# A hybrid decoder layer: the recurrence's scores, turns and outputs on four quadrants of TensorE, and the first input slab computed bank by bank

## The chip, the cores and the metric

The kernel is one launch on one core of a Trainium2 chip. The metric is the device time of that launch in microseconds (us), taken as the median of several runs. The engines are named as the profile names them: PE is TensorE's matmuls and PEld its weight loads, DVE is VectorE, ACT ScalarE, POOL GpSimd, and SP the queue that issues DMAs.

## What is computed

One layer on 1024 tokens of width 1024, all in float32. The input is projected by `w_in`; its columns feed an RWKV-7 group (8 heads of 64, a recurrence over the tokens) and an attention group (8 heads of 64, causal); both results go through `w_out`, a normalisation, a feed-forward part of width 4096 and a second normalisation. The part at issue is the recurrence, one state of 64 x 64 per head:

```python
def step(S, inp):
    r_t, w_t, k_t, v_t, kk_t, a_t = inp
    sa = jnp.einsum('bhvk,bhk->bhv', S, -kk_t)
    S = (S * w_t[:, :, None, :]
         + sa[..., :, None] * (kk_t * a_t)[:, :, None, :]
         + v_t[..., :, None] * k_t[:, :, None, :])
    y = jnp.einsum('bhvk,bhk->bhv', S, r_t)
    return S, y
```

## The kernel before

**The stages.** `input_projection` transposes x on PE (L375), splits it into a high and a low float32r part (`x_hi` by ACT in L483, `x_lo` by DVE in L753), and makes 20 slabs of 128 columns of `x @ w_in`, two per trip. `mla` is the attention, `rwkv_chunks` the recurrence, `mix_ffn` the rest. Every engine has one stream of instructions in each stage, in an order written out by hand, with semaphores between them; PE runs nearly without idle time in all stages.

**The first slab.** The tokens are transposed in two groups of 512. Group g of tile kt goes into PSUM bank kt, from which ACT and then DVE read it. `slab` (L382 to L392) takes two banks, one for each half of the tokens: for each kt three products (high by high, high by low, low by high) into each bank, 48 matmuls in all. Before the first slab PE waits at L379 and L380 for all 16 pieces of `x_lo` and `x_hi`. The slab's banks are 0 and 1.

**The recurrence.** The 1024 tokens are cut into 16 chunks of 64. The 8 heads lie as 4 tiles (`c`, RT = 4) of two halves (`p`): head 2c on partitions 0 to 63, head 2c+1 on 64 to 127 (`own[p]`). Every matmul is 64 x 64 by 64 columns in float32 and leaves two records for the weight load and two for the matmul. Its operands lie on the partitions of its half, and its result goes to the same partitions of a PSUM bank: so half 0 works on the quadrant of the array with rows and columns 0 to 63, half 1 on the one with rows and columns 64 to 127, and the loops alternate between them.

A stage m works on chunk n = m - 1 (`chain`) and prepares chunk m (`ahead`). PE's order in `stage` (L1725 to L1745) is: `product` into B_T1 (8 matmuls, L1721, tile low_t), `rhs_step` (16, L1633 and L1636), `scores_step` (24, L1684 to L1690), `sa_step` (8, L1645), `product` into B_X (8, L1721, tile product), `transposes` (24, L1703, L1706 and L1714), `state_step` (16, L1655 and L1658), `y_step` (24, L1666 to L1672). That is 128 matmuls, so 256 records a stage.

`rhs_step` waits for the scores masked by DVE (`sc_ready`), for v (`v_ready`), for the new state (`state_ready`), and for `y_out`, since its bank B_RY is also the bank of y: `y_leave` (L1776 to L1778) copies y out of it on ACT in one instruction. `tokens_step` (L1780 to L1786) takes the transposes out of two banks in two ACT instructions (v, then b and k). On DVE `mask_step` (L1836 to L1845) takes the scores out of two banks in two instructions, between `rhs_out` (L1820) and `merged` (L1834), which reads bank B_X and updates the inverse; `state_out` (L1824, L1828) follows.

SP loads three matrices for each chunk (`inv_t`, `inv`, `low_t`, two halves each, six DMAs, L1612) into one of three buffer sets; the loads for chunk m are issued after `sa_step` of stage m - 2, and PE's first product of stage m waits for them. At m = 3 four other transfers are issued ahead of the six.

Of the kernel before, what the change touches and what calls it, by code (L numbers as in the profile page):

```python
# [17 lines left out]
ALU = mybir.AluOpType  # L18
# [6 lines left out]
P = 128  # L25
D = 1024
S = 1024
KT = D // P
TT = S // P
HALF = 512  # L30
# [146 lines left out]
def input_projection(nc, mem, k, t, x, w_in, positions):  # L177
# [68 lines left out]
    with ExitStack() as ctx:  # L246
# [119 lines left out]
        def _(pe):  # L366
            mm = nc.tensor.matmul
            pe.wait_ge(consts_in, 16)
            for g in range(2):
                for tt in range(4):  # L370
                    pe.wait_ge(x_in[4 * g + tt], 16)
                    for kt in range(KT):
# [72 lines left out]
            for n in range(TRIPS):  # L445
# [3 lines left out]
                if n in (5, 6):  # L449
                    pe.wait_ge(keys_rooted, n - 4)  # L450
                if n == 6:
                    slab(n, 0, 5, key_sums((2, 3), 1, 6))
                else:
                    slab(n, 0)
# [1075 lines left out]
def rwkv_chunks(nc, mem, k):  # L1530
# [46 lines left out]
    Y0 = RT  # L1577
    cols = lambda c: slice(c * CH, (c + 1) * CH)
    view = lambda bank, n=RT, at=0: ps[:, bank, at * CH:(at + n) * CH].rearrange("p (c n) -> p c n", n=CH)
    now = lambda m: slice(m * CH, (m + 1) * CH)  # L1580

    with ExitStack() as ctx:
# [38 lines left out]
        def _(pe):  # L1621
# [40 lines left out]
            def y_step(n):  # L1662
                q, a = n % 2, n % 3
                for c in range(RT):
                    for p in range(2):
                        mm(ps[own[p], B_RY, cols(Y0 + c)], state[q][own[p], c, :], rd[a][own[p], c, :],  # L1666
                           start=True, stop=False)
                    for p in range(2):
                        mm(ps[own[p], B_RY, cols(Y0 + c)], v_tok[q][own[p], c, :], ks[q][own[p], c, R, :],
                           start=False, stop=False)  # L1670
                    for p in range(2):
                        last = mm(ps[own[p], B_RY, cols(Y0 + c)], u[own[p], c, :], bs[q][own[p], c, :],  # L1672
                                  start=False, stop=True)
                last.then_inc(y_mm, 1)

            def scores_step(m):
                q, a = m % 2, m % 3
                if m >= 1:
                    pe.wait_ge(kd_ready, m)
                    pe.wait_ge(rd_ready, m)  # L1680
                    pe.wait_ge(sc_ready, m)
                for c in range(RT):
                    for p in range(2):
                        mm(ps[own[p], B_KS, cols(2 * c + A_)], kd[q][own[p], c, :], kk_all[own[p], c, now(m)],  # L1684
                           start=True, stop=True)
                    for p in range(2):
                        mm(ps[own[p], B_KS, cols(2 * c + R)], kd[q][own[p], c, :], rd[a][own[p], c, :],
                           start=True, stop=True)
                    for p in range(2):
                        last = mm(ps[own[p], B_B, cols(c)], beta[own[p], c, now(m)], rd[a][own[p], c, :],  # L1690
                                  start=True, stop=True)
                last.then_inc(scores_mm, 1)

            def transposes(m):
# [6 lines left out]
                for c in range(RT):  # L1701
                    for p in range(2):
                        mm(ps[own[p], B_BKT, cols(B * RT + c)], beta[own[p], c, now(m)], k.eye[own[p], :],  # L1703
                           start=True, stop=True)
                    for p in range(2):
                        mm(ps[own[p], B_BKT, cols(K * RT + c)], kd[q][own[p], c, :], k.eye[own[p], :],  # L1706
                           start=True, stop=True)
                if m == 0:
# [3 lines left out]
                for c in range(RT):  # L1712
                    for p in range(2):
                        last = mm(ps[own[p], B_V, cols(c)], hT[own[p], T_V + c, now(m)], centre[own[p], :],  # L1714
                                  start=True, stop=True)
# [38 lines left out]
        def _(act):  # L1754
# [21 lines left out]
            def y_leave(n):  # L1776
                act.wait_ge(y_mm, n + 1)
                A(y_all[:, :, now(n)], view(B_RY, at=Y0), ACT.Copy).then_inc(y_out, 1)  # L1778

            def tokens_step(m):  # L1780
                act.wait_ge(tr_done, m + 1)
                if m >= 2:
                    act.wait_ge(y_mm, m - 1)
                A(v_tok[m % 2][:], view(B_V), ACT.Copy).then_inc(v_ready, 1)
                A(bk_tok[m % 2][:].rearrange("p a c n -> p (a c) n"), view(B_BKT, 2 * RT), ACT.Copy)\
                    .then_inc(tok_ready, 1)  # L1786

# [17 lines left out]
        def _(dve):  # L1805
# [30 lines left out]
            def mask_step(m):  # L1836
                q = m % 2
                dve.wait_ge(scores_mm, m + 1)
                if m >= 2:
                    dve.wait_ge(y_mm, m - 1)  # L1840
                both = mask[:].rearrange("p (o n) -> p o n", o=1).to_broadcast([P, RT, P])
                until = mask[:, CH:P].rearrange("p (o n) -> p o n", o=1).to_broadcast([P, RT, CH])
                V.tensor_tensor(ks[q][:].rearrange("p c a t -> p c (a t)"),
                                ps[:, B_KS, :].rearrange("p (c n) -> p c n", n=P), both, ALU.mult)
                V.tensor_tensor(bs[q][:], view(B_B), until, ALU.mult).then_inc(sc_ready, 1)  # L1845

# [1328 lines left out]
```

## Time and profile before

| | us |
|---|---|
| median of 3 runs (1405.64 to 1410.1) | 1407.78 |
| the profiled execution | 1404.29 |
| its span, first to last instruction | 1402.5 |
| PE busy in the span | 1351.1 |
| DVE busy | 905.5 |
| ACT busy | 454.5 |

A row of a timeline is: start, time covered, engine, line, operation, out<-in, shapes, count, and in brackets the idle time of the engine before it with what ended it. The mean granted clock of TensorE over the span is 0.988 of its full 2.4 GHz. The profiled execution's time is its span and 1.8 us around it.

### The profile page before, as it was taken

What the parts mean: (1) busy time and instruction counts of PE and PEld (TensorE: products, weight loads), DVE (VectorE), ACT (ScalarE), POOL (GpSimd) and SP (SyncE); (2) the same over time, 40 slices, a digit from 0 to 9 for tenths busy, and PEclk for the clock granted to TensorE, in tenths of its full rate; (3) what the DMA queues carried; (4) which work ended last, traced back from release to release, by engine and by line L of the source; (5) the groups of instructions that cost most, each with busy time, mean ns of one, the idle gap of its engine ahead of it and who ended that gap; (6) DMA issues with size and microseconds to landing.
All of it is one profiled execution on the core that took longest, in us unless ns stands there. A gap on an engine that the chain in (4) does not pass through costs nothing.

```text
span 1402.5 us, 23291 instructions
## 1 busy us (share of the span) xinstructions
PE 1351.1 (96%) x9836; PEld 1110.3 (79%) x9836; DVE 905.5 (65%) x995; ACT 454.5 (32%) x623; POOL 495.5 (35%) x310
## 2 busy tenths in 40 slices
PE   6999999998999989997999999999999999999997
PEld 5888787876777769996788887888888888888886
DVE  3538745364555544434758789878776796669877
ACT  2033543132434343332312422221223354433430
POOL 0000212132177400000028577766665364444030
PEclk8999999999999999999999999999999999999999
DMA  5111235387565973232221234444445887565662
GB/s 216 45 46 45 91 128 184 123 184 228 124 185 136 274 225 67 57 86 93 90 89 64 102 126 167 170 141 163 158 158 192 315 290 247 186 199 192 192 203 115
DMA packets 144713, 213.81 MB, mean 152 GB/s; under 512 B 79360, under 2 KB 82048, under 8 KB 143968
## 3 DMA queue, kind: packets, MB, share of 16 engines
q1 hardware_dynamic: 144320, 211.26, 47.3%
q8 instruction: 78, 1.28, 0.4%
q10 hardware_dynamic: 288, 1.05, 0.2%
q14 instruction: 27, 0.22, 0.0%
HBM read 137.75 MB, written 66.39 MB: 146 GB/s over the span
## 4 chain that ended last, share of the span: by engine, by line
PE 49%; DVE 2%; POOL 1%; issue 1%; ACT 0%; DVEq 0%; POOLq 0%; ACTq 0%
PE banks L2441 22%; PE banks L2329 17%; PE banks L2241 6%; PE banks L2317 2%; POOL tile_h L3016 1%; PE banks L2290 1%; POOL tile_s L3016 0%; DVE wout_lo L2672 0%; PE banks L2277 0%; DVE first_relu L2808 0%; PE banks L2268 0%; PE banks L2260 0%; PE banks L2252 0%; DVE y_all L2692 0%; DVE y_all L2688 0%
## 5 line engine op out<-in xcount | busy, mean ns | idle before, releaser
L2441 PE MATMUL banks<-stage_b_hi,stage_a_hi 128*128 128x512 f32 x448 | 174.3, 389 | 0.0
L2441 PE MATMUL banks<-stage_b_lo,stage_a_hi 128*128 128x512 f32 x448 | 174.3, 389 | 0.0
L2441 PE MATMUL banks<-stage_b_hi,stage_a_lo 128*128 128x512 f32 x448 | 174.3, 389 | 0.0
L2836 DVE TENSOR_TENSOR stage_a_lo<-stage_a_raw,stage_a_hi 128x1024 fp32r<-128x1024 f32 x56 | 102.7, 1833 | 37.9 <-ACT stage_a_hi L2602 37.8
L390 PE MATMUL banks<-xT_hi,win_hi 128*128 128x512 f32 x320 | 103.4, 405 | 4.8 <-DVE xT_lo L753 4.8
L390 PE MATMUL banks<-xT_lo,win_hi 128*128 128x512 f32 x320 | 100.4, 395 | 0.0
L390 PE MATMUL banks<-xT_hi,win_lo 128*128 128x512 f32 x320 | 99.9, 394 | 0.0
L2441 PEld LDWEIGHTS banks<-stage_b_hi,stage_a_lo 128*128 128x128 f32 x448 | 84.1, 188 | 17.6
L2441 PEld LDWEIGHTS banks<-stage_b_hi,stage_a_hi 128*128 128x128 f32 x448 | 84.1, 188 | 17.4
L2602 ACT ACTIVATE stage_a_hi<-stage_a_raw 128x1024 fp32r<-128x1024 f32 x56 | 59.4, 1061 | 118.6 <-DMA stage_b_raw<-in_w_ffn 97.0
L2441 PEld LDWEIGHTS banks<-stage_b_lo,stage_a_hi 128*128 128x128 f32 x448 | 84.1, 188 | 17.3
L1362 DVE TENSOR_REDUCE row_max_parts<-banks 128x1 f32<-128x512 f32 (+1 forms) x96 | 50.2, 552 | 42.2 <-PE banks L1144 29.3
L1192 PE MATMUL banks<-probs,v_all 128*128 128x512 f32 (+3 forms) x192 | 74.8, 504 | 2.0 <-ACT probs L1291 2.0
L390 PEld LDWEIGHTS banks<-xT_hi,win_hi 128*128 128x128 f32 x320 | 60.6, 192 | 19.3 <-DVE xT_lo L753 5.1
L390 PEld LDWEIGHTS banks<-xT_lo,win_hi 128*128 128x128 f32 x320 | 61.2, 191 | 13.1
L390 PEld LDWEIGHTS banks<-xT_hi,win_lo 128*128 128x128 f32 x320 | 61.1, 191 | 13.1
L795 POOL COPY norm_wide<-key_norm 128x1024 f32<-128x1024 f32 x4 | 5.1, 1264 | 185.6 <-DVE cum_tile L709 185.6
L1291 ACT ACTIVATE probs<-banks 128x1024 f32<-128x1024 f32 (+3 forms) x64 | 41.4, 650 | 86.6 <-PE banks L1177 50.2
L3040 POOL TENSOR_TENSOR w_slots<-stage_b_raw,w_slots 128x1024 f32<-128x1024 f32 x16 | 44.0, 2755 | 54.7 <-DMA stage_b_raw<-in_w_ffn 52.3
L2987 POOL TENSOR_TENSOR x<-x,ln_gain 128x1024 f32<-128x1024 f32 x7 | 18.6, 2653 | 108.4 <-DMA ln_bias<-in_ln 106.0
L1900 POOL TENSOR_TENSOR k_undecayed<-hT,undecay 128x256 f32<-128x256 f32 x15 | 11.1, 743 | 125.1 <-ACT undecay L1762 125.1
L2839 DVE TENSOR_TENSOR stage_b_lo<-stage_b_raw,stage_b_hi 128x1024 fp32r<-128x1024 f32 x34 | 53.6, 1575 | 0.4
(409 smaller groups left out, 3587.6 us busy)
## 6 DMA issues: line engine op xcount, KB each, us to landing
stage_b_raw<-in_w_ffn SPq DMA_DIRECT2D x50, 512.0 KB, 5.1
stage_a_raw<-hid_s SPq DMA_DIRECT2D x32, 512.0 KB, 4.0
w_landed<-in_w_ffn SPq DMA_DIRECT2D x30, 512.0 KB, 4.8
hid_s<-tile_s SPq DMA_DIRECT2D x60, 256.0 KB, 4.4
stage_a_raw<-hid_h SPq DMA_DIRECT2D x24, 512.0 KB, 4.0
hid_h<-tile_h SPq DMA_DIRECT2D x42, 256.0 KB, 2.0
win_raw<-in_w_in SPq DMA_DIRECT2D x20, 512.0 KB, 3.6
x_tok<-in_x SPq DMA_DIRECT2D x8, 512.0 KB, 7.0
```

What stands on the lines that cost most here:

```text
L390: last = mm(ps[:, 2 * j + b, :], w[j][:, kt, :], r[:, kt, b * HALF:(b + 1) * HALF], start=kt == 0 and i == 0, stop=kt == KT - 1 and i == 2)
L1192: last = mm(ps[:, O[b], lo - b * HALF:HALF], pair[:, 64 * (h % 2):64 * (h % 2) + P], probs[kt % 3][:, lo:(b + 1) * HALF], start=kt == 0, s ...
L1291: A_(probs[kt % 3][:, kt * P:S], flat(T[kt % 2])[:, kt * P:S], ACT.Exp, scale=SCALE)\
L1362: V.reduce_max(tops[:, n, qt:qt + 1], ps[:, b, 0:width], AX_X).then_inc(a_free[b], 1)
L2241: last = nc.tensor.matmul(ps[:, bank + b, :], a[:, kt % RT, tok], w[:, kt, b * HALF:(b + 1) * HALF], start=kt == W_ORDER[0] and n == 0, st ...
L2317: last = nc.tensor.matmul(ps[:, 2 * u + i, :], a[:, j, at], b, start=kt == 0 and n == 0, stop=kt == KT - 1 and n == 2)
L2329: last = nc.tensor.matmul(ps[:, bank_of(u, name), :], a[:, j, cut], b(kt), start=kt == 0 and n == 0, stop=kt == HK - 1 and n == 2)
L2441: last = nc.tensor.matmul(ps[:, bank, :], s[a][:, j, tok], s[b][:, j, :], start=p == 0 and j == 0 and n == 0, stop=p == NP - 1 and j == 1 ...
L2602: A(s["a_hi"][:], s["a_raw"][:], COPY).then_inc(hi2, 1)
L2836: V.tensor_tensor(s["a_lo"][:], s["a_raw"][:], s["a_hi"][:].bitcast(F32), ALU.subtract).then_inc(lo2, 1)
L2839: V.tensor_tensor(s["b_lo"][:], src, s["b_hi"][:].bitcast(F32), ALU.subtract).then_inc(lo2, 1)
L3040: G.tensor_tensor(dst, a, b, ALU.subtract).then_inc(combined, 1)
```

## The change

Three helpers place results. `out_half(c, p)` gives the partitions of a result: the matmul's own half for an even tile c, the other half for an odd one. `score_bank(c)` and `token_bank(c)` give a different bank to even and odd tiles. `scores_step`, `transposes` and `y_step` go through the tiles two at a time, so that four matmuls in a row are meant for four different quadrants. `rhs_step`, `sa_step`, `state_step` and both products stay as they were. What odd tiles write into the other half must be brought back: each evicting instruction becomes three, one for the even tiles on all 128 partitions, and one for each half of the odd tiles. `y_step` now also writes bank B_X, so it waits for `merged` of the next chunk (`xt_up`). The first slab is computed by a function of its own: first bank 0 for all kt, then bank 1, with a wait for the pieces of `x_lo` that each step needs.

```diff
-            pe.wait_ge(xlo_done, 2 * KT)
-            pe.wait_ge(xhi_done, 2 * KT)
+            def first_slab():
+
+                pe.wait_ge(w_split[0], 1)
+                for b in range(2):
+                    for kt in range(KT):
+                        pe.wait_ge(xlo_done, KT + max(kt * b + 1, b + 1))
+                        for i, (w, r) in enumerate(((w_hi, x_hi), (w_hi, x_lo), (w_lo, x_hi))):
+                            last = mm(ps[:, b, :], w[0][:, kt, :], r[:, kt, b * HALF:(b + 1) * HALF],
+                                      start=kt == 0 and i == 0, stop=kt == KT - 1 and i == 2)
+                last.then_inc(slab_mm[0], 1)
...
+    other = (own[1], own[0])
+    out_half = lambda c, p: (own, other)[c % 2][p]
+    score_bank = lambda c: (B_KS, B_B)[c % 2]
+    token_bank = lambda c: (B_BKT, B_V)[c % 2]
+    part_of = lambda rows, bank, at, n: ps[rows, bank, at * CH:(at + n) * CH]
+
+    def by_tiles(dst, banks, at, n):
+
+        yield dst(slice(0, P), slice(0, RT, 2)), part_of(slice(0, P), banks[0], at, n)
+        for p in range(2):
+            yield dst(own[p], slice(1, RT, 2)), part_of(other[p], banks[1], at, n)
...
             def y_step(n):
                 q, a = n % 2, n % 3
+                if n < NC_ - 1:
+                    pe.wait_ge(xt_up, n + 2)
+                for j in range(0, RT, 2):
+                    four = [(c, p) for c in (j, j + 1) for p in range(2)]
+                    to = lambda c, p: ps[out_half(c, p), (B_RY, B_X)[c % 2], cols(Y0 + j // 2)]
+                    for c, p in four:
+                        mm(to(c, p), state[q][own[p], c, :], rd[a][own[p], c, :], start=True, stop=False)
...
             def scores_step(m):
...
+                for j in range(0, RT, 2):
+                    four = [(c, p) for c in (j, j + 1) for p in range(2)]
+                    for c, p in four:
+                        mm(ps[out_half(c, p), score_bank(c), cols(j + A_)], kd[q][own[p], c, :],
+                           kk_all[own[p], c, now(m)], start=True, stop=True)
...
             def y_leave(n):
                 act.wait_ge(y_mm, n + 1)
-                A(y_all[:, :, now(n)], view(B_RY, at=Y0), ACT.Copy).then_inc(y_out, 1)
+                for dst, src in by_tiles(lambda rows, cs: y_all[rows, cs, now(n)], (B_RY, B_X), Y0, 2):
+                    last = A(dst, src.rearrange("p (c n) -> p c n", n=CH), ACT.Copy)
+                last.then_inc(y_out, 1)
...
             def tokens_step(m):
...
-                A(v_tok[m % 2][:], view(B_V), ACT.Copy).then_inc(v_ready, 1)
...
+                for dst, src in by_tiles(lambda rows, cs: v[rows, cs, :], (B_BKT, B_V), RT, 2):
+                    last = A(dst, src.rearrange("p (c n) -> p c n", n=CH), ACT.Copy)
+                last.then_inc(v_ready, 1)
+                for dst, src in by_tiles(lambda rows, cs: bk[rows, :, cs, :], (B_BKT, B_V), 0, 4):
+                    last = A(dst, src.rearrange("p (a c n) -> p a c n", a=2, n=CH), ACT.Copy)
+                last.then_inc(tok_ready, 1)
...
             def mask_step(m):
...
+                for (dst, src), rows in zip(by_tiles(lambda rows, cs: ks[q][rows, cs, :, :], (B_KS, B_B), 0, 4), halves):
+                    n = rows.stop - rows.start
+                    V.tensor_tensor(dst.rearrange("p c a t -> p c (a t)"), src.rearrange("p (c n) -> p c n", n=P),
+                                    both(rows).to_broadcast([n, 2, P]), ALU.mult)
+                for (dst, src), rows in zip(by_tiles(lambda rows, cs: bs[q][rows, cs, :], (B_KS, B_B), RT, 2), halves):
...
```

## Rows read from the trace of the kernel before

**Rows 1.** The page: busy time, share of the span and instructions of TensorE.
```profile
PE 1351.1 (96%) x9836; PEld 1110.3 (79%) x9836; DVE 905.5 (65%) x995; ACT 454.5 (32%) x623; POOL 495.5 (35%) x310
```
**Rows 2.** One stretch: PE, PEld, DVE, ACT, POOL busy, clock, DMA share, GB/s.
```profile
518.00:635.00 117.00, 112.51 (x3684) 110.08 (x3680) 49.61 (x111) 36.73 (x97) 9.60 (x14) 1.00 0.31 78
```
**Rows 3.** Timeline of the matmuls, one stage of the recurrence.
```profile
541.53 0.33 PE L1633 MATMUL banks<-v_tok,k_scores 64*64 64x64 f32 x4
...
542.48 0.31 PE L1684 MATMUL banks<-kk_all,k_undecayed 64*64 64x64 f32 x4
...
543.88 0.66 PE L1645 MATMUL banks<-rhs,inverse_t 64*64 64x64 f32 x16
...
544.82 0.31 PE L1703 MATMUL banks<-eye,beta_all 64*64 64x64 f32 x4
...
547.16 0.22 PE L1666 MATMUL banks<-r_decayed,state 64*64 64x64 f32 x1
...
548.56 0.22 PE L1721 MATMUL banks<-inverse,low_t 64*64 64x64 f32 x1
...
549.34 0.33 PE L1633 MATMUL banks<-v_tok,k_scores 64*64 64x64 f32 x4
```
**Rows 4.** Timeline of the matmuls where L1706 hands over to L1714.
```profile
537.89 0.22 PE L1714 MATMUL banks<-centre,hT 64*64 64x64 f32 x1
537.95 0.22 PE L1706 MATMUL banks<-eye,k_undecayed 64*64 64x64 f32 x1
```
**Rows 5.** Timeline of the matmuls, a weight load of 128 columns for two.
```profile
134.00 1.84 PE L149 MATMUL banks<-ones_block,key_square 128*128 128x2 f32 x16
135.70 0.72 PE L390 MATMUL banks<-xT_hi,win_hi 128*128 128x512 f32 x2
```
**Rows 6.** Timeline of ScalarE in the stage of rows 3.
```profile
546.45 0.38 ACT L1784 ACTIVATE v_tok<-banks 128x256 f32<-128x256 f32 x1 [1.48 <-PE banks L1714]
546.73 0.59 ACT L1785 ACTIVATE bk_tok<-banks 128x512 f32<-128x512 f32 x1
548.82 0.38 ACT L1778 ACTIVATE y_all<-banks 128x256 f32<-128x256 f32 x1 [1.50 <-PE banks L1672]
```
**Rows 7.** Timeline of VectorE in the stage of rows 3.
```profile
542.71 0.42 DVE L1820 COPY rhs<-banks 128x256 f32<-128x256 f32 x1 [1.03 <-PE banks L1636]
544.11 0.69 DVE L1843 TENSOR_TENSOR k_scores<-banks,mask 128x512 f32<-128x512 f32 x1 [0.97 <-PE banks L1690]
544.72 0.41 DVE L1845 TENSOR_TENSOR b_scores<-banks,mask 128x256 f32<-128x256 f32 x1
545.05 0.44 DVE L1834 COPY_PREDICATED inverse_t<-own_merge,banks 128x256 f32<-128x256 int32 x1
547.41 0.42 DVE L1824 TENSOR_TENSOR state_sum<-state,banks 128x256 f32<-128x256 f32 x1 [1.92 <-PE banks L1658]
```
**Rows 8.** TensorE's waits, 507 to 645 us: total, times, longest.
```profile
PE banks L1721 <- DMA low_t<-low_d: 1.6, 1, 1.6
```
**Rows 9.** Timeline of the SP queue in the stage of rows 3.
```profile
544.58 1.23 SPq L1612 DMA_DIRECT2D inverse_t<-inv_t_d  x2
...
547.17 2.14 SPq L1612 DMA_DIRECT2D low_t<-low_d  x2
```
**Rows 10.** The line L1612, all its DMAs.
```profile
DMA to landing us min/median/max: 2.2/2.7/5.9
```
**Rows 11.** Timeline of the matmuls at the first slab.
```profile
24.95 1.22 PE L390 MATMUL banks<-xT_hi,win_hi 128*128 128x512 f32 x2 [4.83 <-DVE xT_lo L753]
...
30.80 0.62 PE L390 MATMUL banks<-xT_hi,win_lo 128*128 128x512 f32 x2
...
33.99 0.39 PE L390 MATMUL banks<-xT_hi,win_hi 128*128 128x512 f32 x1
```
**Rows 12.** Timeline of VectorE before the first slab.
```profile
20.02 4.88 DVE L753 TENSOR_TENSOR xT_lo<-banks,xT_hi 128x512 fp32r<-128x512 f32 x8 [2.71 <-ACT xT_hi L483]
```
**Rows 13.** One stretch at the first slab, columns as in rows 2.
```profile
22.60:29.40 6.80, 4.45 (x11) 3.49 (x12) 4.28 (x8) 0.82 (x2) 0.00 (x0) 0.50 0.20 55
```

More of the change, by code:

```diff
@@ L1663, in y_step @@
                 q, a = n % 2, n % 3
[L1664 to L1673, printed above, removed]
+                if n < NC_ - 1:
[6 more added lines that the diff above has]
+                    for c, p in four:
+                        mm(to(c, p), v_tok[q][own[p], c, :], ks[q][own[p], c, R, :], start=False, stop=False)
+                    for c, p in four:
+                        last = mm(to(c, p), u[own[p], c, :], bs[q][own[p], c, :], start=False, stop=True)
                 last.then_inc(y_mm, 1)
@@ L1681, in scores_step @@
                     pe.wait_ge(sc_ready, m)
[L1682 to L1691, printed above, removed]
+                for j in range(0, RT, 2):
+                    four = [(c, p) for c in (j, j + 1) for p in range(2)]
+                    for c, p in four:
+                        mm(ps[out_half(c, p), score_bank(c), cols(j + A_)], kd[q][own[p], c, :],
+                           kk_all[own[p], c, now(m)], start=True, stop=True)
+                    for c, p in four:
+                        mm(ps[out_half(c, p), score_bank(c), cols(j + R)], kd[q][own[p], c, :],
+                           rd[a][own[p], c, :], start=True, stop=True)
+                    for c, p in four:
+                        last = mm(ps[out_half(c, p), score_bank(c), cols(RT + j // 2)], beta[own[p], c, now(m)],
+                                  rd[a][own[p], c, :], start=True, stop=True)
                 last.then_inc(scores_mm, 1)
@@ L1700, in transposes @@
                     pe.wait_ge(values_left, 2)
[L1701 to L1707, printed above, removed]
+                for j in range(0, RT, 2):
+                    four = [(c, p) for c in (j, j + 1) for p in range(2)]
+                    for c, p in four:
+                        mm(ps[out_half(c, p), token_bank(c), cols(2 * B + j // 2)], beta[own[p], c, now(m)],
+                           k.eye[own[p], :], start=True, stop=True)
+                    for c, p in four:
+                        mm(ps[out_half(c, p), token_bank(c), cols(2 * K + j // 2)], kd[q][own[p], c, :],
+                           k.eye[own[p], :], start=True, stop=True)
                 if m == 0:
@@ L1713, in transposes @@
                     for p in range(2):
-                        last = mm(ps[own[p], B_V, cols(c)], hT[own[p], T_V + c, now(m)], centre[own[p], :],
+                        last = mm(ps[out_half(c, p), token_bank(c), cols(RT + c // 2)], hT[own[p], T_V + c, now(m)],
+                                  centre[own[p], :],
                                   start=True, stop=True)
@@ L1783, in tokens_step @@
                     act.wait_ge(y_mm, m - 1)
[L1784 to L1786 removed]
+                v, bk = v_tok[m % 2], bk_tok[m % 2]
+                for dst, src in by_tiles(lambda rows, cs: v[rows, cs, :], (B_BKT, B_V), RT, 2):
[4 more added lines that the diff above has]
+                last.then_inc(tok_ready, 1)
             A(k.att_sum[own[0], :], ps[own[0], B_BKT, :], ACT.Copy).then_inc(sums_left, 1)
```

16 lines of the change are left out of this document (10 added, 6 removed).

## The prediction

> **What bounds the kernel.** I read the page's busy times first: PE is busy 96% of the span [rows 1]. Then the stretch of the recurrence by itself: 112.5 us of 117 are PE's, DVE has under half, and the granted clock is full, 2.4 GHz [rows 2]. So a change pays only where it shortens PE's stream or a wait of PE.
>
> The timeline of one stage says what sets the pace. A stage lasts from one rhs to the next, 549.34 - 541.53 = 7.81 us. Its 48 records of scores run from 542.48 to 543.88, 29.2 ns a record; the 48 of y take 548.56 - 547.16 = 1.40 us, the same [rows 3]. Two quadrants take turns, so one quadrant takes a record each 58 ns. Is that the quadrant or PE's issue? A record of L1714 starts 0.06 us before the last of L1706, which stands ahead of it in the program [rows 4]: the halves are two streams, each at its own pace, and neither waits for the order of the other. So it is the quadrant. Inside one, load and matmul overlap: 16 loads of 128 columns with hardly anything to stream take 135.70 - 134.00 = 1.70 us, 0.106 each [rows 5]; for 64 columns that is some 0.053 (an estimate, half of it), and with a stream of about the same after it a record would need more than the 0.058 seen.
>
> 256 records at 29.2 ns are 7.47 us of the 7.81. The other 0.3 is one wait: y's last record starts just ahead of 548.56, ACT starts y_leave at 548.82 and ends 0.38 later, and rhs starts at 549.34, 0.14 after that; of these 0.78 us the 16 records of the B_T1 product fill 0.47 [rows 3, 6].
>
> **The recurrence, part by part.**
> 1. Scores, transposes and y, 144 records of 256, move to four quadrants. At best four streams at 58 ns each: 14.6 ns a record, 144 x 14.6 = 2.10 us off a stage. The trace shows no two matmuls that share rows but not columns, so the pace must be bounded. Lower end 14.6. Upper ends: 29.2, if a half of the rows serves one quadrant at a time; and 55.5, if moreover a load doesn't overlap the other quadrant's stream ((0.053 + 0.058) / 2). I take 14.6, because rows 4 show streams without a common order and a load that overlaps a stream in the same rows is what each of them already does [rows 3 to 5].
> 2. y_leave becomes three ACT instructions of 128 columns. From 256 to 512 columns ACT goes from 0.38 to 0.59 us, and the next starts 0.28 after one of 256 [rows 6]. So 128 columns: 0.275 long, 0.175 apart; the last ends at 2 x 0.175 + 0.275 = 0.625 in place of 0.38. rhs waits for it, in a wait that is exposed: +0.25.
> 3. Shorter scores uncover rhs_out. DVE starts it 542.71 - 541.53 = 1.18 after rhs and takes 0.42 [rows 7]; with 0.14 to PE, sa can start at 1.74. PE reaches it at 0.93 (32 records of rhs) + 0.70 = 1.63: +0.11.
> 4. mask_step becomes six instructions. DVE's spacing is 0.61 for 512 columns, 0.33 for 256 [rows 7], so 0.19 for 128: 3 x 0.33 + 3 x 0.19 = 1.56 for 0.94. It starts 0.23 after the scores, at 1.86, ends its spacing at 3.42, and merged (0.44) ends at 3.86. y now waits for merged, and would start at 1.74 + 0.47 + 0.47 + 0.70 + 0.93 = 4.31: hidden, with 0.3 to spare after the way to PE. If it came late, y alone would wait, and behind it the next product. Then state_out (its first part 0.25 after the state's last matmul, 547.41 [rows 7]; about 0.9 in all) ends at 5.4, before y_out.
> 5. tokens_step becomes six: 3 x 0.175 + 3 x 0.28 = 1.37 for 0.79 or so. It starts 0.25 after the transposes (3.38), at 3.63, and ACT is free at 5.0. y ends at 4.31 + 0.70 = 5.01 and y_leave starts at 5.26: hidden by 0.2 us. Without that cover it would fall on the wait of point 2.
> 6. POOL's k_undecayed needs only exps, as before, and has a whole stage. SP's six loads of a stage are issued in 549.31 - 544.58 = 4.73 us [rows 9] and land 2.7 later at the median [rows 10], so about 7.5 after sa ends at 2.2: 9.7. The product that needs them starts 2 x 6.0 - 1.0 = 11 after the same zero: hidden, with 1.3 us. It isn't in the first stages: stage 1's product already waits for low_t [rows 8], so nothing ahead of it gains; and at m = 3 four transfers (0.65 each, 2.6) go ahead of the six. sa_mm of stage 1 is then at 2.2, the last of the six is issued at 2.4 + 2.6 + 4.1 = 9.1 and lands up to 5.9 later; taken at 4.5 (between median and maximum) 13.6, against a need at 11.2: 2.3 us lost, once.
>
> New stage: 5.01 to y's end, and 0.78 + 0.25 to rhs: 6.04, so 1.77 less. Fifteen such stages 26.6, less 2.3, plus 0.5 in the last stage (y 0.7 shorter, y_leave 0.25 longer): **24.8 us**.
>
> **The first slab.** PE idles 4.83 us until 24.95 for x_lo [rows 11], though bank 0 needs only the first piece of the second group: DVE starts it at 20.02, one of eight in 4.88 us [rows 12], so done at about 20.7; PE starts at 20.8, 4.1 earlier. Bank 0's 24 matmuls, at (33.99 - 30.80) / 14 = 0.228 [rows 11], last until 26.3, after the last x_lo (24.9): bank 1 waits for nothing, and the second slab's weights are split by 26.8, long before 31.7. Besides, the granted clock stands at 0.50, that is 1.2 GHz, from 22.6 to 29.4 [rows 13], after PE had stood idle from about 20.1. 11 records in that stretch came each 0.427 apart in place of 0.228: 2.2 us. With the gap closed to 0.7 us I expect the clock to stay up; if it falls all the same, 16 records of bank 0 and 1 run slow instead and only 3.1 of the total is left. **6.3 us**, 3.1 at worst. It carries on to the end, since what follows is PE's own stream.
>
> **Sum.** 24.8 + 6.3 = 31.1. The sum is made in the profiled execution, 1404.29 (span 1402.5 and 1.8 around it), which lies 3.5 below the median; I take it off the median: 1407.8 - 31.1 = 1376.7.
>
> **The rivals.** All share the first slab's -6.3. Less than 0.3% (4.2 us) can't be told from no change here.
> - **A, four full streams**, above: 1377; 1368 (early loads cost nothing, no wait of point 3) to 1385 (points 4 and 5 exposed by 0.3 us a stage, or the clock falls).
> - **B, issue sets a floor.** Two instructions a record have never come faster than 29.2 ns here, so PE's fetch or issue may not give one in 14.6. Halfway, 22 ns: 144 x 7.2 = 1.04 less, 0.25 more, 15 x 0.79 = 12; 1390, between 1385 and 1401. Against it: rows 4's starts 0.06 apart out of order say that a queue stands ahead of the array, and a load and a matmul every 29.2 ns make at most 14.6 an instruction.
> The Trainium skill, page "TensorE: Matmul & The Clock Gate", section "Wait — 56ns, not 53.3ns?", states that start to start never drops below about 25 ns, however small the matmul. By that rule (an estimate from that page) a stage would save 0.60 - 0.25 and the kernel some 11 us. The trace can't bear it out: no stretch of it is free of the quadrant's 58 ns.
> - **C, a half of the rows serves one quadrant at a time.** The pace stays at 29.2; only the longer y_leave is left, 15 x 0.25 = 3.7, against the slab's 6.3: 1405. For it: the trace has no such pair at work.
> - **D, slower: a load waits for the stream of the other quadrant with the same rows.** Then the pace is 55.5: 144 x 26.3 = 3.8 us a stage, 16 x 3.8 + 3.7 - 6.3 = +58, 1466. It decides from where the pace passes 29.2 + (6.3 / 15 - 0.25) / 144 = 30.4 ns; beyond 32.3 it is slower by over 0.3%. Against it: loads overlap streams in one quadrant already [rows 3, 5].
> The same page of the Trainium skill, "TensorE: Matmul & The Clock Gate", section "The mechanism", says that a weight load overlaps a running matmul only if the row groups differ. The pace of one quadrant here contradicts the plain form of it; for two quadrants in the same rows no row shows it.
>
> **Chances.** A 0.62, B 0.18, C 0.12, D 0.08. The likeliest is A: 1376.7. The range 1368 to 1407 holds A, B and C and leaves out D and A's tail. Faster by over 0.3%: A and B, 0.80; within: C, 0.12; slower: D, 0.08.
>
> **What would show it.** In the timeline of a stage, 48 records of L1684 to L1690's successors in 0.70 us (A), about 1.05 (B), 1.40 (C), 2.7 (D); rhs to rhs 6.0 us; PE idle before rhs about 0.56, released by y_all; ACT's three y instructions ending 0.6 after the first starts; no wait on xt_up before y; a wait of about 2 us on L1612 at the third product; L390's successor starting at 20.8 at full clock. I am wrong about the hidden parts if PE waits at y for merged, at rhs for v_tok, or in a middle stage for low_t; wrong about the sum if the stage gains 1.8 and a later part of the kernel gives it back.

## The result, and the profile after

The changed kernel takes 1401.12 us (median of 12 runs, 1395.81 to 1405.69), the kernel before beside it 1407.68 us (12 runs): ratio 0.995, 95% interval 0.9935 to 0.9964, so 6.6 us faster where 31 were forecast. Behind the first slab the profiled execution lies 6.2 us ahead of the one before, as forecast. The recurrence, which was to bring 24.8, brought about nothing: its 15 stages, from the first sums (L1655, before L1633) to the last, took 122.1 us before and take 121.1. One pair of executions shows no more than that: their lead of 6.2 us is 3.7 at the first sums, 4.6 at the last and 3.0 at the end of the span, against 6.6 in the medians. The granted clock may be a part of it: here TensorE stood at 1.2 GHz for 10.2 us between 504 and 529 us (0.80 on average), where the kernel before kept 2.4 in its whole recurrence.

```profile
504.00:529.00 25.00, 18.04 (x607) 17.39 (x611) 12.88 (x32) 10.93 (x32) 2.41 (x3) 0.80 0.57 152
```

The page's busy line of TensorE, and the same stretch of the recurrence as [rows 2], answering to [rows 1, 2]:

```profile
PE 1325.7 (95%) x9836; PEld 1082.7 (77%) x9836; DVE 920.5 (66%) x1059; ACT 478.4 (34%) x719; POOL 496.5 (35%) x310
```
```profile
518.00:635.00 117.00, 86.97 (x3680) 82.93 (x3676) 66.16 (x167) 59.19 (x186) 9.46 (x13) 0.99 0.30 75
```

PE's work shrank by 25.5 us in this stretch (112.5 to 87.0) and as many records (3684 and 3680) still fill the 117 us. The time is not in the work; it is in gaps. The timeline of the matmuls of one stage shows two of them (last column: idle time before the row, and what ended it):

```profile
585.03 0.33 PE L1655 MATMUL banks<-v_tok,k_scores 64*64 64x64 f32 x4 [0.99 <-ACT y_all L1805]
...
585.90 0.27 PE L1708 MATMUL banks<-kk_all,k_undecayed 64*64 64x64 f32 x2
...
586.08 0.30 PE L1711 MATMUL banks<-r_decayed,k_undecayed 64*64 64x64 f32 x6
...
586.43 0.30 PE L1711 MATMUL banks<-r_decayed,k_undecayed 64*64 64x64 f32 x6
...
586.69 0.68 PE L1667 MATMUL banks<-rhs,inverse_t 64*64 64x64 f32 x16
...
588.14 0.28 PE L1739 MATMUL banks<-centre,hT 64*64 64x64 f32 x3
589.43 0.39 PE L1739 MATMUL banks<-centre,hT 64*64 64x64 f32 x11 [1.02 <-issue]
...
590.48 0.27 PE L1692 MATMUL banks<-r_decayed,state 64*64 64x64 f32 x2
...
591.26 0.66 PE L1747 MATMUL banks<-inverse,low_t 64*64 64x64 f32 x16
592.97 0.33 PE L1655 MATMUL banks<-v_tok,k_scores 64*64 64x64 f32 x4 [1.05 <-ACT y_all L1805]
```

The scores take 0.79 us and y 0.78, in place of 1.40 each [rows 3]; inside them the four streams come 14.6 ns a record (24 records from 586.08 to 586.43). But the stage is 7.94 us long. PE stands idle for 1.05 us until the outputs have left, and for 1.02 us in the middle of the centring matmuls, where nothing the profile shows holds it ("issue"). ScalarE and VectorE in the same stage, answering to [rows 6, 7]:

```profile
589.93 0.84 ACT L1814 ACTIVATE v_tok<-banks 128x128 f32<-128x128 f32 x3 [2.13 <-PE banks L1739]
590.80 1.16 ACT L1817 ACTIVATE bk_tok<-banks 128x256 f32<-128x256 f32 x3
591.99 0.84 ACT L1805 ACTIVATE y_all<-banks 128x128 f32<-128x128 f32 x3
```
```profile
586.95 1.29 DVE L1878 TENSOR_TENSOR k_scores<-banks,mask 128x256 f32<-128x256 f32 x3 [0.31 <-PE banks L1714]
588.25 0.89 DVE L1882 TENSOR_TENSOR b_scores<-banks,mask 128x128 f32<-128x128 f32 x3
589.18 0.44 DVE L1866 COPY_PREDICATED inverse_t<-own_merge,banks 128x256 f32<-128x256 int32 x1
```

The tokens' eviction ends at 591.96, after y's last matmul, so the outputs leave late. TensorE's waits from 514 to 630 us (total, times, longest):

```profile
PE banks L1655 <- ACT y_all L1805: 12.1, 14, 1.1
PE banks L1739 <- issue: 4.6, 6, 1.1
PE banks L1728 <- issue: 3.7, 2, 3.1
PE banks L1711 <- issue: 2.8, 2, 2.4
PE banks L1677 <- issue: 1.9, 2, 1.4
PE banks L1680 <- issue: 1.8, 2, 1.3
PE banks L1731 <- issue: 1.7, 2, 0.8
```

Two causes, then: 12.1 us in 14 waits for the outputs, and 16.5 in 16 waits on "issue" whose place moves through the stage. Counting the records gives the second a rule: the matmul that ends such a gap is record 4257, 4510, 4763, 5016, 5269, 5522 of the kernel, one in every 253, which is 506 loads and matmuls. The kernel before had three gaps of this kind, at records 2865, 2992 and 6028 (1.2, 0.3 and 1.3 us).

The two causes take turns. By the starts of the records from 3751 to 5775, eight times 253, the first 127 of each, in which the wait for the outputs falls, take 4.1 us on average, and the 126 behind them, which end in a gap on "issue", 3.5. In the kernel before the same halves take 4.1 and 3.8.

The first slab, answering to [rows 11, 13]:

```profile
20.87 0.47 PE L387 MATMUL banks<-xT_hi,win_hi 128*128 128x512 f32 x1 [0.57 <-DVE xT_lo L764]
...
31.87 0.62 PE L399 MATMUL banks<-xT_hi,win_hi 128*128 128x512 f32 x2
```
```profile
22.60:29.40 6.80, 6.80 (x32) 5.62 (x31) 4.29 (x8) 0.83 (x2) 0.00 (x0) 1.00 0.26 57
```

It starts 4.1 us earlier, the granted clock stays at 2.4 GHz where it had been at 1.2, and PE has no gap.

### The profile page after: what moved, and what is told of

Same layout as the page of the kernel before. It is cut to its first block, busy times and chain, and to the rows that moved or that the text cites. A ratio compares the mean times of both kernels' runs of the same rounds, so it can differ in the third digit from the quotient of the medians.

```text
span 1399.5 us, 23451 instructions
## 1 busy us (share of the span) xinstructions
PE 1325.7 (95%) x9836; PEld 1082.7 (77%) x9836; DVE 920.5 (66%) x1059; ACT 478.4 (34%) x719; POOL 496.5 (35%) x310
## 3 DMA queue, kind: packets, MB, share of 16 engines
q10 hardware_dynamic: 288, 1.05, 0.2%
## 4 chain that ended last, share of the span: by engine, by line
PE 49%; DVE 2%; POOL 1%; issue 1%; ACT 0%; DVEq 0%; POOLq 0%; ACTq 0%
PE banks L2480 22%; PE banks L2368 17%; PE banks L2280 6%; PE banks L2356 2%; POOL tile_h L3055 1%; PE banks L2329 1%; POOL tile_s L3055 0%; DVE wout_lo L2711 0%; PE banks L2316 0%; DVE first_relu L2847 0%; PE banks L2307 0%; PE banks L2299 0%; PE banks L2291 0%; DVE y_all L2731 0%; DVE y_all L2727 0%
## 5 line engine op out<-in xcount | busy, mean ns | idle before, releaser
L2875 DVE TENSOR_TENSOR stage_a_lo<-stage_a_raw,stage_a_hi 128x1024 fp32r<-128x1024 f32 x56 | 99.3, 1772 | 41.1 <-ACT stage_a_hi L2641 41.1
L2641 ACT ACTIVATE stage_a_hi<-stage_a_raw 128x1024 fp32r<-128x1024 f32 x56 | 59.4, 1061 | 119.9 <-DMA stage_b_raw<-in_w_ffn 99.9
L399 PE MATMUL banks<-xT_hi,win_hi 128*128 128x512 f32 x304 | 97.4, 402 | 0.0
L399 PE MATMUL banks<-xT_lo,win_hi 128*128 128x512 f32 x304 | 94.5, 393 | 0.0
L399 PE MATMUL banks<-xT_hi,win_lo 128*128 128x512 f32 x304 | 94.2, 391 | 0.0
L399 PEld LDWEIGHTS banks<-xT_hi,win_hi 128*128 128x128 f32 x304 | 57.0, 190 | 13.5 <-issue 2.4
L399 PEld LDWEIGHTS banks<-xT_lo,win_hi 128*128 128x128 f32 x304 | 57.6, 190 | 12.2
L399 PEld LDWEIGHTS banks<-xT_hi,win_lo 128*128 128x128 f32 x304 | 57.6, 190 | 12.2
```

The source lines that it names most:

```text
L399: last = mm(ps[:, 2 * j + b, :], w[j][:, kt, :], r[:, kt, b * HALF:(b + 1) * HALF], start=kt == 0 and i == 0, stop=kt == KT - 1 and i == 2)
L2641: A(s["a_hi"][:], s["a_raw"][:], COPY).then_inc(hi2, 1)
L2875: V.tensor_tensor(s["a_lo"][:], s["a_raw"][:], s["a_hi"][:].bitcast(F32), ALU.subtract).then_inc(lo2, 1)
```

## The experiments

Two theories. **Eviction**: the token and output evictions, each cut into three instructions, make ACT's chain too long. **Supply**: PE's instructions reach it at a rate that holds the stage, whatever PE has to do; a matmul of the recurrence is two records, each a load and a matmul, so four instructions. A third, **traffic**, has the loads of the base matrices hold up the instructions' transfers. "15 stages" is the distance from the first to the last sums of the recurrence in the profiled execution, one for each kernel, so differences of 1 or 2 us in it say little. For the ratios the kernel before was timed again beside each, with medians of 1407.9 to 1409.3 us. e7 leaves out loads that the computation needs and e10 and e11 a part of it, so their outputs are not the layer's; e9 and e14 were run once each.

| kernel | quadrants | matmuls a stage | 15 stages, us | median, us | ratio to before, 95% interval |
|---|---|---|---|---|---|
| before | 2 | 128 | 122.1 | 1407.7 | |
| after | 4 | 128 | 121.1 | 1401.1 | 0.9950, 0.9935 to 0.9964 |
| e1 slab only | 2 | 128 | 123.0 | 1401.2 | 0.9948, 0.9929 to 0.9967 |
| e2 quadrants only | 4 | 128 | 123.7 | 1408.1 | 1.0008, 0.9990 to 1.0027 |
| e3 merged scores | 4 | 120 | 118.5 | 1397.5 | 0.9923, 0.9899 to 0.9948 |
| e4 outputs early | 4 | 128 | 122.0 | 1402.4 | 0.9959, 0.9939 to 0.9978 |
| e5 split, before | 2 | 152 | 144.3 | 1436.5 | 1.0188, 1.0168 to 1.0207 |
| e6 split, after | 4 | 152 | 146.6 | 1425.9 | 1.0119, 1.0102 to 1.0137 |
| e7 no loads | 4 | 128 | 119.6 | 1399.0 | 0.9931, 0.9910 to 0.9952 |
| e8 e3 and e4 | 4 | 120 | 118.1 | 1398.0 | 0.9916, 0.9894 to 0.9937 |
| e10 fewer instructions | 4 | 112 | 112.3 | 1388.8 | 0.9868, 0.9832 to 0.9904 |
| e11 fewer, outputs early | 4 | 112 | 115.1 | 1389.3 | 0.9856, 0.9808 to 0.9905 |
| e12 112 matmuls | 4 | 112 | 113.4 | 1394.6 | 0.9904, 0.9882 to 0.9926 |
| e13 e12, outputs early | 4 | 112 | 111.9 | 1394.7 | 0.9899, 0.9877 to 0.9920 |
| e15 slab and merged scores | 2 | 120 | 119.9 | 1396.6 | 0.9933, 0.9909 to 0.9956 |

**e1, the first slab alone**, and **e2, the quadrants alone**. The edit is one half of the diff each.

> The kernel before with the new first slab alone. All theories put the slab's own gain at about 6.2 us, the distance by which the second slab starts earlier in the profile after. If the recurrence on four quadrants is worth nothing in the end, this kernel stands level with the whole change: 1401 to 1402 us. If the recurrence gains some us and a later loss hides it, this kernel is slower than the whole change; if four quadrants cost time, it is the fastest of the three, under 1400 us.

> The whole change without the new first slab. Supply theory (PE's instructions arrive at a rate that holds a stage above about 7.3 us) and eviction theory (ACT's tokens and outputs in thirds end too late for the next stage) both see a recurrence within 2 us of the kernel before: 1405 to 1408 us. If the two parts of the change work against each other (the earlier start shifts where the clock falls), it is under 1402 us.

e1 stands level with the whole change, e2 with the kernel before. The two parts don't help or hurt each other: the gain is the first slab's, as far as intervals of 3 to 5 us can tell.

**e3, two products in one.** kk and the decayed r are laid out so that one operand reaches both:

```diff
-                        mm(ps[out_half(c, p), score_bank(c), cols(j + A_)], kd[q][own[p], c, :],
-                           kk_all[own[p], c, now(m)], start=True, stop=True)
-                    for c, p in four:
-                        mm(ps[out_half(c, p), score_bank(c), cols(j + R)], kd[q][own[p], c, :],
-                           rd[a][own[p], c, :], start=True, stop=True)
+                        mm(part_of(out_half(c, p), score_bank(c), j, 2).rearrange("p (a n) -> p a n", a=2),
+                           kd[q][own[p], c, :], kk_and_rd(c, p, m), start=True, stop=True)
```

> The whole change, with the two score products that share a stationary operand issued as one of 128 columns: 8 of 128 matmuls of a stage fewer, the same columns, evictions and waits. Supply theory: a stage has 6% fewer PE instructions and falls by 0.35 to 0.45 us, the whole by 5 to 7 us, and the gaps that came every 253 PE records come every 253 records still, so less than one a stage. Eviction theory: no PE wait that sets the end changes; the time stays within 1 us of the whole change, 1400 to 1402 us.

3.6 us less than the whole change, under the 5 to 7 that supply expected; the intervals of the two overlap, so it speaks for supply without settling it. One such record of 128 columns takes as long as two of 64 (28 to 30 ns on four quadrants), so PE's work is nearly the same.

**e4, the outputs early.**

```diff
                 last.then_inc(v_ready, 1)
+                if m:
+                    y_leave(m - 1)
                 for dst, src in by_tiles(lambda rows, cs: bk[rows, :, cs, :], (B_BKT, B_V), 0, 4):
```

> The whole change, with ACT evicting the outputs of the last chunk between the v tokens and the k and b tokens of the next. Eviction theory: the sums' wait for the outputs (0.8 to 1.3 us a stage) shrinks by the 1.16 us of the k and b tokens, bounded by the end of the output products: a stage falls by 0.6 to 0.8 us, the whole by 9 to 12 us, to about 1390 us. Supply theory: that wait lies in the shadow of the instructions' arrival; PE stands at its record gaps instead, which grow to 1.5 us or more, and a stage can't fall under 7.3 us: at most 4 us in all, 1397 to 1401 us.

The outputs now leave before the k and b tokens, and PE's wait for them fell by 4.2 us; the gaps on "issue" grew from 16.7 to 19.5 (all rows of both views), with new ones at records 4890 and 5396, 127 after the old ones at 4763 and 5269. Waits of e4, 514 to 630 us:

```profile
PE banks L1655 <- ACT y_all L1805: 7.9, 14, 0.6
PE banks L1739 <- issue: 7.3, 6, 1.4
PE banks L1677 <- issue: 4.6, 3, 2.4
```

The eviction theory wanted 9 to 12 us and got none: 1402.4, also 1.4 above the supply's range. The new gaps are not explained to the end: behind record 4763 the next packet of instructions (e9 shows what these are) sets out 2.2 us after PE has resumed, behind the same record of the whole change 1.2, and in e9 1.0 to 1.1.

**e5 and e6, the scores in halves.** Each of the 24 score products becomes two of 32 columns, in the kernel before and in the changed one:

```diff
+                    half = lambda x, h, at=0: x[own[p], c, at + 32 * h:at + 32 * h + 32]
-                    for c, p in four:
-                        mm(ps[out_half(c, p), score_bank(c), cols(j + R)], kd[q][own[p], c, :],
-                           rd[a][own[p], c, :], start=True, stop=True)
+                    for h in range(2):
+                        for c, p in four:
+                            mm(to(c, p, j + R, h), kd[q][own[p], c, :], half(rd[a], h), start=True, stop=True)
```

> The kernel before, with each of the 24 score products of a stage issued as two of 32 columns: 152 matmuls instead of 128, the same columns, evictions and waits. Supply theory: the instructions of a stage grow by 19%, so its least length goes from 7.3 to about 8.6 us, over the 7.8 that the engine needs: 11 to 14 us slower, 1419 to 1423 us, with gaps of about 1 us every 253 PE records, which the kernel before showed hardly at all. Engine theory (a stage is as long as its columns and waits): if half the columns take half the time (14.6 ns a record) nothing changes, 1407 to 1409 us; if a record of 32 columns takes as long as one of 64, the scores take 1.4 us more a stage and the kernel is 21 us slower, without such gaps.

> The whole change, with the same split of its score products. Supply theory: a stage grows by 19% of 7.6 us, 1.2 to 1.4 us, the whole by 17 to 21 us, to 1418 to 1422 us, the same as the split kernel before, although this one's PE has 1.8 us less work in a stage. Eviction theory: the scores on four quadrants take 0.7 us more a stage at most (14.6 ns a record whatever its columns): 1401 to 1412 us.

In e5 a record of 32 columns takes as long as one of 64 (30 ns on two quadrants, 15 on four), so PE itself became slower and hid the supply: 27.6 us more, almost without gaps, nearer the second branch of the engine theory (21) than to supply's 11 to 14. e6 is the better test. The window 514 to 630 us of e5, then of e6, columns as in [rows 2]:

```profile
514.00:630.00 116.00, 113.24 (x3551) 111.23 (x3550) 41.93 (x93) 31.49 (x84) 9.01 (x13) 0.95 0.28 68
```
```profile
514.00:630.00 116.00, 82.83 (x3651) 78.39 (x3648) 57.09 (x143) 50.20 (x158) 9.69 (x13) 0.99 0.26 63
```

PE is busy 98% of the one and 71% of the other, and 15 stages take as long (144.3 and 146.6). e6 is 24.8 us slower than the whole change, above supply's 17 to 21 and far above the 0 to 11 of eviction. A part of e5's 144.3 is the granted clock (0.95 on average, e6 0.99): most of its stages take 9.18 us, those in the middle of e6 9.5 on average.

**e7, no loads.** `for x, dst in (..) if m < 4 else ()`: the base matrices are loaded for the first four chunks only.

> The whole change, with the chunks' three matrices (inverse transposed, inverse, lower part) loaded for the first four chunks alone; later chunks compute on those again. The wait for the lower part of about 2.5 us in the third stage stays. Traffic theory (the loads hold up the instruction fetches): fetches of 16 KB fall from 0.9 to 1.4 us to about 0.9 all, the record gaps fall to half, a stage falls by 0.4 us or more, the whole by 5 us or more: under 1396 us. Supply theory: most of the time from one fetch to the next isn't the transfer; a stage falls by 0.1 to 0.2 us, 1398 to 1401 us. Eviction theory: no change, 1400 to 1402 us.

2.1 us less than the whole change; the DMA share of the stretch fell from 0.31 to 0.13, and the gaps are still there. As the cause of the gaps the traffic of these loads falls, but for those 2 us.

```profile
514.00:630.00 116.00, 87.52 (x3775) 83.65 (x3773) 67.99 (x173) 58.72 (x185) 10.15 (x14) 0.99 0.13 38
```

The loads that e7 leaves in place are another matter. The longest gaps of the whole change, 2.4 us at record 2865 and 3.1 at 6028, have 0.8 and 0.9 MB of other transfers in and just before them (v and the gates, then `w_out`), and two of the kernel before's three gaps stand at the same records. That the large transfers lengthen them is likely, but no run took these away.

**e8, e3 and e4 together.**

> The whole change with the merged score products and the early eviction of the outputs together. Supply theory: with fewer instructions the gaps shrink, so a part of the shorter output wait is kept: 0 to 3 us less than the merged products alone, 1394 to 1398 us. Eviction theory: the 0.6 us a stage of the early outputs, 1391 us or less.

No different from e3, as supply had it.

**e9 and e14, a burst with nothing to wait for.** 24 more copies of the first chunk's score products stand ahead of the counted ones, on four quadrants (e9, in the changed kernel) or on two (e14, in the kernel before).

> The whole change with 24 extra copies of the first chunk's score products, on four quadrants, without a wait, before the counted ones: 576 matmuls, 1152 PE records. Engine theory: all run at the 14.6 ns a record of the bursts seen, 16.8 us from first to last, and the kernel is about 17 us longer. Supply theory: only the first 250 to 500 records run at that pace, then the engine stands about 1 to 2 us every 253 or 256 records, with two instruction fetches of 16 KB for each such stretch, 3.3 to 3.9 us apart: 28 to 34 us from first to last, the kernel 28 to 34 us longer. Here no semaphore and no other engine can cause a gap.

This shows a limit of supply by itself. Four windows of e9, columns as in [rows 2], two stretches of matmuls and the two gaps behind them:

```profile
517.82:519.70 1.88, 1.88 (x128) 1.88 (x128) 0.00 (x0) 0.00 (x0) 0.00 (x0) 1.00 0.03 9
519.71:521.26 1.55, 0.20 (x15) 0.07 (x6) 0.00 (x0) 0.00 (x0) 0.00 (x0) 1.00 0.00 0
521.27:523.14 1.87, 1.86 (x126) 1.86 (x128) 0.00 (x0) 0.00 (x0) 0.00 (x0) 1.00 0.03 9
523.17:524.72 1.55, 0.20 (x15) 0.07 (x5) 0.00 (x0) 0.00 (x0) 0.00 (x0) 1.00 0.00 0
```

128 records, 256 instructions, run at 14.6 ns each at full clock, and then PE is idle. The timeline of the matmuls, only the rows with idle time before them:

```profile
514.09 0.28 PE L1779 MATMUL banks<-r_decayed,beta_all 64*64 64x64 f32 x4 [1.91 <-issue]
...
517.82 0.28 PE L1779 MATMUL banks<-kk_all,k_undecayed 64*64 64x64 f32 x4 [1.64 <-issue]
...
521.27 0.28 PE L1779 MATMUL banks<-r_decayed,k_undecayed 64*64 64x64 f32 x4 [1.36 <-issue]
...
524.73 0.28 PE L1779 MATMUL banks<-r_decayed,beta_all 64*64 64x64 f32 x4 [1.36 <-issue]
...
528.18 0.28 PE L1779 MATMUL banks<-kk_all,k_undecayed 64*64 64x64 f32 x4 [1.36 <-issue]
```

(528.18 - 514.09) / 4 = 3.52 us for 256 instructions; over the six periods up to 535.64 it is 3.59. A gap stands at every 128th record, twice as often as the theory had written down. What arrives in between stands in the DMA view from 516 to 536 us (40 slices of 0.5 us):

```profile
GB/s 0 0 0 0 0 33 0 0 0 0 0 0 33 0 0 0 0 0 0 33 0 0 0 0 0 0 33 0 0 0 0 0 0 0 33 0 0 0 0 0
DMA packets 5, 0.08 MB, mean 4 GB/s; under 512 B 0, under 2 KB 0, under 8 KB 0
...
q8 instruction: 5, 0.08, 1.7%
```

The only traffic is the instruction queue's, one packet of 16 KB per gap. By the trace's DMA records a packet sets out 1.0 to 1.1 us after PE resumes, is under way 0.9 to 1.3, and PE resumes 1.3 to 1.5 after its end. The 1152 records take 32.0 us (504.8 to 536.8) in place of 16.8, and the kernel takes 1432.7.

The Trainium skill, page "Runtime: NRT & Kernel Launch", section "Instruction fetch mechanics", has instructions come in blocks of 16 KB, 256 of them, through a DMA queue of the engine's own, at a cost "mostly hidden". The trace agrees on the block. It isn't hidden here: the gaps are 1.4 to 1.9 us of every 3.6.

> The kernel before with 24 extra copies of the first chunk's score products on two quadrants, 1152 PE records without a wait. If two streams take 29 to 30 ns a record whatever is supplied, 1152 records take 34 us with no gap over 0.2 us, and a fetch comes every 3.75 us: as long as the 31 to 32 us that e9 took on four quadrants plus 2 or 3, so that four quadrants were worth under a tenth of a long stretch. If supply were no limit for four quadrants outside their gaps, or the two quadrants too showed gaps, the burst is over 36 us.

The same burst on two quadrants takes 35.4 us (509.2 to 544.6), without a gap, and the kernel 1441.1. The whole, and its two parts by the clock:

```profile
509.20:544.60 35.40, 35.40 (x1157) 35.40 (x1156) 1.10 (x3) 0.80 (x2) 0.00 (x0) 0.94 0.16 41
509.20:513.20 4.00, 4.00 (x81) 4.00 (x80) 1.10 (x3) 0.80 (x2) 0.00 (x0) 0.50 0.73 201
513.30:544.60 31.30, 31.30 (x1080) 31.30 (x1078) 0.00 (x0) 0.00 (x0) 0.00 (x0) 1.00 0.09 20
```

The first 4 us ran at 1.2 GHz, which is why it is over the 34 us of the forecast; from then on two quadrants take 29.2 ns a record at 2.4 GHz. The first 3.5 us of e9 were at 1.2 GHz too, so the totals are 35.4 and 32.0, a tenth apart. At full clock 128 records take 3.73 us on two quadrants, and one period of e9 3.59: doubling the pace of the array shortens a stretch without waits by 4%. The kernel before ran just above the supply's limit.

**e10 and e11, fewer instructions.** `range(0, 0 if m > 1 else RT, 2)` leaves out the transposes of beta and the decayed keys.

> The whole change without the 16 transposes of beta and the decayed keys in chunks 2 to 15 (112 matmuls a stage instead of 128); their evictions and waits stay. The output is then not the reference's. Supply theory: a stage falls by up to an eighth, 0.96 us, 10 to 13 us in all, unless the outputs' eviction then sets it: 1388 to 1396 us. Eviction theory: the tokens' eviction starts 0.5 us earlier, so the wait for the outputs shrinks by that much: 6 to 7 us, 1394 to 1395 us; the record gaps are as many as before.

> The same, with the outputs evicted early as in e4. Supply theory: now that the instructions leave room, the earlier outputs are worth something that they were not in the whole change: 2 to 5 us less than e10. Eviction theory: 9 to 12 us less than e10. If neither holds and the outputs are worth nothing here too, the same as e10.

e10 is at 1388.8 us, in supply's range (1388 to 1396) and 5 us under eviction's. It takes 0.47 us of PE's work out of a stage as well as instructions, so by itself it separates the two less well than e6. e11 is the same, where both theories wanted something of it; the third case that was written down fits, an earlier eviction of the outputs gains nothing that four runs between 1383.5 and 1395.8 could show.

**e12 and e13, the full computation in 112 matmuls.** The transpose of beta joins its scores as e3's products do, and the k and v tokens leave together:

```diff
-                        mm(ps[out_half(c, p), token_bank(c), cols(2 * B + j // 2)], beta[own[p], c, now(m)],
-                           k.eye[own[p], :], start=True, stop=True)
...
-                        last = mm(ps[out_half(c, p), score_bank(c), cols(RT + j // 2)], beta[own[p], c, now(m)],
-                                  rd[a][own[p], c, :], start=True, stop=True)
+                            last = mm(part_of(out_half(c, p), score_bank(c), RT + j, 2)
+                                      .rearrange("p (a n) -> p a n", a=2),
+                                      beta[own[p], c, now(m)], eye_and_rd(c, p, m), start=True, stop=True)
```

> The whole change with the same products and transposes in 112 matmuls a stage instead of 128: the scores with kk and with the decayed r share one matmul, and the transpose of beta shares one with its scores; the k and v tokens leave in one eviction, the beta tokens in another. Supply theory: an eighth fewer instructions, a stage of 7.2 to 7.3 us as in e10, so 1389 to 1393 us, 9 to 12 us less than the whole change. Eviction theory: v tokens now leave with the k tokens (0.3 us later), the outputs no earlier: 1400 to 1405 us.

> The same, with the outputs evicted ahead of the beta tokens. Supply theory: within 2 us of e12, as e11 was of e10, since a shorter wait moves into the gaps. Eviction theory: 6 us or more less than e12.

1394.6 us, 13.3 less than the kernel before beside it and with an interval of the ratio below that of the whole change: this version beats both. It lies 2 us above the forecast's range. The window and the longest waits of e12, 514 to 630 us:

```profile
514.00:630.00 116.00, 90.62 (x3422) 85.52 (x3414) 69.20 (x176) 61.82 (x194) 9.51 (x13) 1.00 0.31 78
```
```profile
PE banks L1674 <- ACT y_all L1836: 9.9, 14, 1.0
PE banks L1711 <- issue: 2.4, 3, 1.9
PE banks L1778 <- issue: 2.4, 2, 1.4
```

What an instruction costs can be read only roughly from the table. From 152 to 112 matmuls a stage (e6 to e12), 160 instructions less, the stage falls by (146.6 - 113.4) / 15 = 2.21 us, 3.54 us per 256, near the period of the burst. The two halves of the way don't agree: from 152 to 128 it is 4.5 us per 256 (e6's split also adds 0.7 us of PE's work to a stage), from 128 to 112 it is 2.1. e13, like e11, shows no gain from the early outputs.

**e15, fewer instructions on two quadrants.** e1 and e3's merged products.

> The kernel before with the new first slab (e1) and with the merged score products of e3, on two quadrants as before: 120 matmuls a stage. If two streams held the kernel before (30 ns a record of 64 columns, twice that for one of 128), it stands with e1: 1400 to 1402 us, PE with hardly a gap. If the arrival of instructions held it already, it gains what e3 gained on the whole change, 3 to 5 us: 1396 to 1398 us.

1396.6, in the range of supply, but its trace is that of two full streams: PE without gaps in the middle, all middle stages 7.72 us, where e1 has most at 7.78 and some at 7.9 to 8.2. 0.06 a stage are PE's (four records of 128 columns take 0.22 us, eight of 64 took 0.235, four times a stage), the rest are short stalls of supply that e1 had now and then. The six runs fall into four at 1396.5 and two at 1402, and e1's own twelve go from 1396.5 to 1406.3, so how large the gain is stays open. It fits with two limits that lay side by side in the kernel before, and doesn't show it by itself.

## Why the prediction was wrong

- **The first slab** (forecast 6.3, at worst 3.1): right, number and mechanism. Start at 20.87 for 20.8, full clock, second slab at 31.87 for 31.7; e1 is 7.6 us under the kernel before, interval 4.6 to 10.
- **Point 1, the pace**: right as a pace, 14.6 ns a record on four quadrants; rivals C and D fell, and e9 shows it over 128 records in a row. **This is the step that failed**: the one from the pace to the stage, the "144 x 14.6 = 2.10 us off a stage" and with it the "New stage: 6.04". It took PE's instructions to be there whenever the array was free. They are not: 512 at 3.59 us per 256 are 7.2 us, and the stage came to 7.68 in the middle of the recurrence (stages 4 to 13 of the 15). The 0.5 above 7.2 lie in the other halves of the stages, 4.1 us of PE's work and its wait for the outputs where the halves that end in a gap take 3.5.
- **Rival B** had the mechanism, PE's fetch, at 0.18, with the wrong form and price. It was taken as a floor of 22 ns under each record, where e9 shows a rate over blocks: bursts at 14.6, then a gap. The sentence put against it, that one load and one matmul every 29.2 ns "make at most 14.6 an instruction", held the number that mattered: the supply is 3.59 / 256 = 14.0 ns an instruction, so the kernel before had 4% to spare and no more. The time fell at the very end of B's own range and was inside the whole one because that was drawn wide for C, a wrong mechanism: luck.
- **The floor of about 25 ns** that the Trainium skill states (page "TensorE: Matmul & The Clock Gate", section "Wait — 56ns, not 53.3ns?") does not show as a pace between different quadrants: e9 has 14.6 ns from record to record in every burst.
- **Point 2, y_leave**: +0.25 forecast. Three evictions of 128 columns end 0.84 after the first starts, not 0.62: the spacing is 0.28, as for 256 columns, so the extrapolation from 512 and 256 down to 128 was wrong. +0.46.
- **Point 4, mask_step**: 1.56 forecast, 589.18 - 586.95 = 2.23 measured; six spacings of 0.43 and 0.31, where 0.33 and 0.19 had been taken. merged still ends before y begins (589.62, 590.48), but only since the gap of 1.02 had held PE back; in e10, with fewer gaps, y waits for it 3.8 us in 6 stages:

```profile
PE banks L1692 <- DVE inverse_t L1866: 3.8, 6, 0.7
```

- **Point 5, the tokens**: forecast hidden by 0.2 us, measured late. They take 2.06 for 1.37, and start 4.9 us after the sums, not 3.63, because the gap stands ahead of them. PE's wait for the outputs is 1.05. By e4, e8, e11 and e13 an earlier eviction gains nothing that the runs could tell from zero; in e4 other gaps grew by more than this wait fell.
- **Point 3**: DVE's eviction of the sums did not hold sa but in one stage. **Point 6**: in the middle no load was late, and e7 leaves 2.1 us for all of them together. The 2.3 us that were to be lost at the third product were not; stage 1's product waited 2.5 us for `low_t` in place of 1.6 (e7's expectation puts this wait in the third stage by mistake).

## What to carry to other kernels

Before speeding up a long unrolled stretch of small matmuls, count its instructions per microsecond: here TensorE was fed 256 in about 3.6 us, and float32 matmuls of 64 columns on two quadrants already use 96% of that. Past that point more quadrants bought nothing, and fewer, wider instructions did; matmuls that share a stationary operand are the ones to join. Where PE stands on "issue", number the records that end the gaps: gaps a fixed count of records apart point to the supply. A wait elsewhere in the stage may then be worth less than its length: test it before mending it.

## What the runs showed that was not expected

- TensorE's supply of instructions: bursts of exactly 128 records, a packet of 16 KB and a gap of 1.36 to 1.91 us each; 3.45 to 3.73 us a period (e9), with all other DMA silent in all but the first. What fills the time outside the packet's 0.9 to 1.3 us is open.
- A 64x64 record takes as long for 32 columns as for 64 (e5, e6), and one for 128 columns takes twice that (on four quadrants in e3, on two in e15: 0.22 us for four).
- Four quadrants of 64x64 run at once, 14.6 ns from record to record (e9), though each shares its rows with one other and its columns with another.
- ACT and DVE read a bank at a spacing that hardly falls below 256 columns: ACT 0.28 us at 128 as at 256 [rows 6], DVE 0.31 at 128, and 0.43 at 256 in this layout where it had been 0.33.
